# A two-block transformer on one core: the matmuls' moving operands as contiguous chunks, read and written every fourth 16-byte line in four rounds, with new gaps ahead of the two weight tiles

## The reference

```python
z = h @ w_in[l]                              # 2048 -> 10248 columns
merged = gc * (conv_y @ w_conv_out[l]) + ga * (attn @ w_attn_out[l])
x = x + merged @ w_mix_out[l]
u = jnp.square(jax.nn.relu(rmsnorm(x, g_mlp[l]) @ w_ff1[l]))   # 8192 wide
x = rmsnorm(x + u @ w_ff2[l], g_final)
...
proj = h @ w_in_2[l]                         # second block, 5648 columns
x = x + gate_m * (concat(attn, ssm) @ w_out_2[l])
x = x + gate_f * conv_ffn(h, w_up_2[l], conv_ffn_w_2[l], conv_ffn_b_2[l], w_down_2[l])
out = rms_norm(x, final_norm_g_2)
```

## Time and profile before

| | |
|---|---|
| median of 3 runs | 2444.2 us (2444.05 to 2444.67) |
| the profiled execution, its span | 2444.7 us |
| TensorE matmul (PE) busy | 2423.8 us, 99%, 14373 matmuls |
| TensorE weight load (PEld) busy | 2149.2 us, 88% |
| VectorE (DVE) busy | 1969.0 us, 81% |
| ScalarE (ACT) busy | 1261.4 us, 52% |
| GpSimd (POOL) busy | 89.1 us, 4% |
| DMA | 566.81 MB, mean 232 GB/s |

### The profile page before, as it was taken

The page is one execution under the profiler, slowest core; times in us unless marked ns, Lnnn a source line. Parts: engine busy times, 40 slices in busy tenths (PEclk is TensorE's granted clock), DMA queues, the critical chain, the costliest instruction groups (busy, mean ns, idle before and its releaser), DMA issues.

```text
span 2444.7 us, 47745 instructions
## 1 busy us (share of the span) xinstructions
PE 2423.8 (99%) x14373; PEld 2149.2 (88%) x14373; DVE 1969.0 (81%) x3114; ACT 1261.4 (52%) x2038; POOL 89.1 (4%) x109
## 2 busy tenths in 40 slices
PE   8999999999999999999999999999999999999998
PEld 7888888888888888888888988889888888888887
DVE  7778876689987887887898877776887887887886
ACT  6444445565554454554555555565545445445455
POOL 0000001000000000000000105300000000000000
PEclk9999999999999999999999999999999999999999
DMA  7786885657888888888888555555566656656555
GB/s 275 274 282 211 279 284 192 200 190 268 285 292 293 287 291 292 286 293 291 289 288 281 175 177 194 188 171 190 167 187 200 202 180 198 198 178 212 192 176 169
DMA packets 162812, 566.81 MB, mean 232 GB/s; under 512 B 18883, under 2 KB 19452, under 8 KB 162748
## 3 DMA queue, kind: packets, MB, share of 16 engines
q1 hardware_dynamic: 132572, 458.71, 56.4%
q10 hardware_dynamic: 27792, 101.20, 12.5%
q0 software_dynamic: 2384, 6.09, 1.0%
HBM read 563.51 MB, written 2.42 MB: 231 GB/s over the span
## 4 chain that ended last, share of the span: by engine, by line
PE 77%; DVE 4%; issue 2%; ACT 1%; DVEq 0%; DMA 0%; ACTq 0%; SPq 0%
PE bank L334 77%; DVE w_lo L1345 1%; DVE scratch L1994 0%; DVE scratch L1992 0%; DVE scratch L1351 0%; DVE scratch L1997 0%; ACT w_hi L823 0%; DMA w_raw<-in_w_in 0%; DVE Z L1705 0%; DVE H L1714 0%; DVE scratch L2020 0%; ACT U L1297 0%; DVE scratch L2014 0%; DVE scratch L1378 0%; PE bank L678 0%
## 5 line engine op out<-in xcount | busy, mean ns | idle before, releaser
L1345 DVE TENSOR_TENSOR w_lo<-w_raw,w_hi 128x1024 fp32r<-128x1024 f32 (+2 forms) x898 | 1048.0, 1176 | 117.1 <-ACT w_hi L823 107.5
L334 PE MATMUL bank<-H,w_hi 128*128 128x512 f32 (+1 forms) x4480 | 1100.0, 386 | 9.3 <-ACT w_hi L275 8.1
L334 PEld LDWEIGHTS bank<-H,w_hi 128*128 128x128 f32 x4480 | 799.3, 188 | 136.7 <-issue 11.2
L823 ACT ACTIVATE w_hi<-w_raw 128x1024 fp32r<-128x1024 f32 (+2 forms) x898 | 876.4, 1012 | 24.1 <-PE bank L334 8.4
L334 PEld LDWEIGHTS bank<-H,w_lo 128*128 128x128 f32 x4416 | 591.5, 188 | 40.5
L334 PE MATMUL bank<-H,w_lo 128*128 128x256 f32 x4416 | 602.9, 277 | 0.0
L334 PE MATMUL bank<-U,w_hi 128*128 128x512 f32 (+1 forms) x2011 | 501.7, 384 | 0.5 <-DVE U L2022 0.3
L853 ACT ACTIVATE scratch<-bank 128x256 f32<-128x256 f32 x355 | 135.1, 381 | 669.3 <-PE bank L334 668.7
L334 PEld LDWEIGHTS bank<-U,w_hi 128*128 128x128 f32 x2011 | 351.1, 188 | 50.0 <-DVE U L2022 0.6
L334 PEld LDWEIGHTS bank<-U,w_lo 128*128 128x128 f32 x1984 | 275.3, 188 | 23.7
L334 PE MATMUL bank<-U,w_lo 128*128 128x256 f32 x1984 | 282.1, 277 | 0.0
(11 more groups left out here) (246 smaller groups left out, 1113.2 us busy)
## 6 DMA issues: line engine op xcount, KB each, us to landing
w_raw<-in_w_ff SPq DMA_DIRECT2D x256, 512.0 KB, 5.0
ada_w<-in_w_ada ACTq DMA_DIRECT2D x192, 512.0 KB, 4.7
w_raw<-in_w_up SPq DMA_DIRECT2D x176, 512.0 KB, 4.5
w_raw<-in_w_z SPq DMA_DIRECT2D x96, 512.0 KB, 4.8
w_raw<-in_w_in SPq DMA_DIRECT2D x88, 512.0 KB, 4.4
w_raw<-in_w_gate SPq DMA_DIRECT2D x64, 512.0 KB, 4.6
w_raw<-in_w_down SPq DMA_DIRECT2D x64, 384.0 KB, 3.2
w_raw<-in_w_down SPq DMA_DIRECT2D x64, 320.0 KB, 3.4
```

Of the source, the lines that this page charges most:

```text
L334: return nc.tensor.matmul(out, lhsT, rhs, start=start, stop=stop, skip_group_check=True)
L823: A(w_hi[:, slot, 0:cols], w_raw[:, slot, 0:cols], ACT.Copy).then_inc(sem("w_high"), 1)
L1345: TT(w_lo[:, slot, 0:cols], w_raw[:, slot, 0:cols], w_hi[:, slot, 0:cols].bitcast(F32), ALU.subtract)\
```

## The change

H, U and B become plain contiguous areas of 16 chunks of 128 lines. All matmuls of `mm_lines` now walk through a chunk in four rounds: first lines 0, 4, 8 and so on, then 1, 5, 9 and so on, then from 2 and from 3; the output is walked in the same way (four numbers, skip twelve, four rounds), so that each result lands where it did. A matmul of 512 columns has rounds of 32 lines, one of 256 columns rounds of 16. Number, shape, order and semaphores of all instructions stay. H, U, B and G, Z are placed with a gap of 1024 numbers between H and U (the chains of before reached beyond the area there), and the small tiles R and ss move into that gap. Unused tiles of 11 and 6 lines stand ahead of `w_hi` and `w_lo`; a tile starts at a multiple of two lines, so the first becomes a gap of 12 lines.

```diff
-STEP = 3
 LINES = 2 * T // LINE
-CHAIN_N = NC * 2 * T + (STEP - 1) * 2 * T
+AREA_N = NC * 2 * T
+GAP = 1024
+HIGH_SPACE, LOW_SPACE = 11, 6
...
-            area = nc.alloc_sbuf_tensor_at(name, [P, CHAIN_N], F32R, offset=base + at)
-            return bass.AP(area[:, :].tensor, LINE, [[CHAIN_N, P], [2 * T, NC], [STEP * LINE, LINES], [1, LINE]])
+            area = nc.alloc_sbuf_tensor_at(name, [P, AREA_N], F32R, offset=base + 4 * at)
+            return area[:, :].rearrange("p (k l e) -> p k l e", k=NC, e=LINE)
...
-        U = chunks_by_line("U", NC * 2 * T * 4)
-        B = chunks_by_line("B", 2 * NC * 2 * T * 4)
+        U = chunks_by_line("U", AREA_N + GAP)
+        B = chunks_by_line("B", 2 * AREA_N + GAP)
...
         w_raw = sb("w_raw", [P, 4, PIECE])
+        sb("space_hi", [P, HIGH_SPACE * LINE])
         w_hi = sb("w_hi", [P, 4, PIECE], F32R)
+        sb("space_lo", [P, LOW_SPACE * LINE])
         w_lo = sb("w_lo", [P, 4, PIECE], F32R)
...
-        R = sb("R", [P, T])
-        ss = sb("ss", [P, T])
+        R = nc.alloc_sbuf_tensor_at("R", [P, T], F32, offset=base + 4 * AREA_N)
+        ss = nc.alloc_sbuf_tensor_at("ss", [P, T], F32, offset=base + 4 * (AREA_N + T))
...
+        def in_turn_of_lines(ap):
+
+            return ap.rearrange("p (i a) e -> p a i e", a=4)
...
             def mm_lines(out, lhsT, rhs, start, stop):
-                return mm(lines(out), lhsT, rhs, start, stop)
+
+                return mm(in_turn_of_lines(lines(out)), lhsT, in_turn_of_lines(rhs), start, stop)
```

More of the change, by code:

```diff
@@ L107, in build @@
         base = (nc.sbuf_base + 31) // 32 * 32
-        ctx.enter_context(nc.sbuf_tensor("arena", [P, 3 * NC * 2 * T + 1024 + (Z_BLOCKS - 32) * T], F32))
+        ctx.enter_context(nc.sbuf_tensor("arena", [P, 3 * AREA_N + GAP + (Z_BLOCKS - 32) * T], F32))
         def sb(name, shape, dt=F32):
@@ L121, in chunks_by_line @@
         def chunks_by_line(name, at):
-            area = nc.alloc_sbuf_tensor_at(name, [P, CHAIN_N], F32R, offset=base + at)
-            return bass.AP(area[:, :].tensor, LINE, [[CHAIN_N, P], [2 * T, NC], [STEP * LINE, LINES], [1, LINE]])
+            area = nc.alloc_sbuf_tensor_at(name, [P, AREA_N], F32R, offset=base + 4 * at)
+            return area[:, :].rearrange("p (k l e) -> p k l e", k=NC, e=LINE)
         H = chunks_by_line("H", 0)
-        U = chunks_by_line("U", NC * 2 * T * 4)
-        B = chunks_by_line("B", 2 * NC * 2 * T * 4)
-        G = nc.alloc_sbuf_tensor_at("G", [P, NC, 2, T], F32, offset=base + NC * 2 * T * 4 + 4096)
-        Z = nc.alloc_sbuf_tensor_at("Z", [P, Z_BLOCKS, T], F32, offset=base + 2 * NC * 2 * T * 4 + 4096)
+        U = chunks_by_line("U", AREA_N + GAP)
+        B = chunks_by_line("B", 2 * AREA_N + GAP)
+        G = nc.alloc_sbuf_tensor_at("G", [P, NC, 2, T], F32, offset=base + 4 * (AREA_N + GAP))
+        Z = nc.alloc_sbuf_tensor_at("Z", [P, Z_BLOCKS, T], F32, offset=base + 4 * (2 * AREA_N + GAP))
         X = sb("X", [P, NC, T])
```

## The result

The changed kernel takes 2483.82 us (2483.56 to 2485.14, median of 4), the kernel before 2444.43 us beside it. The ratio is 1.0162, with a 95% interval of 1.0147 to 1.0176. The forecast was 2405 us; the range, 2350 to 2535, holds the result, the sign is wrong. The profiled execution has a span of 2482.1 us. In all runs of these kernels a span is 1.7 to 1.9 us shorter than its time (here 2483.96 and 2482.1), so the profiled execution of the kernel before, with a span of 2444.7, took some 2446.5 us (an estimate), 2 us above its median; the spans of the two traces therefore differ by 2 us less than the times.

A forecast was written before the change was run, and what follows sets the result against it. TensorE's matmul pace was taken as the bound, 2345 us of 2444.7. Half of the stream's 79 us loss was taken as removed, 2444.2 - 39 = 2405 us, other parts at no cost; range 2350 to 2535.

The forecast's parts named there:

- the sign: Whole kernel: forecast faster, 2444.2 - 39 = 2405 us; chances faster 0.58, same 0.10, slower 0.32.
- distances at no price: Operand against weight tiles: distances change, no row says which is good; the 39 us forecast gain gives them no term.
- half of the stream's loss: All large matmuls: the new line order removes half of the 79 us lost along the stream, 39 us.
- `narrow` row: Matmuls with only four lines of weights, 0.227 us each: taken to show weight-load collision is not most of the loss.
- the 11.5 ns: Each 512-column matmul: 0.2248 us against 0.2133 at 2.4 GHz, a loss put down to the full pace of asking for lines.
- Reading four apart collides more: Rival, matmul reads: lines four apart meet each other and the weight load; 2450 to 2529 us, middle 2490; chance 0.24.
- `keep_warm` as the price of straight reading: Matmuls reading contiguous lines: if four apart were as bad, 0.233 us per 512 columns, 85 us together, 2529 us.
- Parts at no cost: Outside matmul pace: no instruction, wait, DMA or queue position added or moved; ScalarE and VectorE writes become contiguous; nothing.
- The pace is the same: Matmul pace in three stages: the same under different DMA, VectorE and ScalarE loads, so not set by their memory work.
- VectorE as cover: Tightest stretch: VectorE, idle 0.23 to 0.24 us a unit, can follow to about 5.2 us, covering the forecast.
- Writing in pieces: Rival, matmul result writes: 16-byte pieces cost 5% of the stream, 117 us, giving 2561 us; chance 0.08.

The follow-up runs named there:

- 11 and 11: Changed kernel with high and low weight tiles both 11 lines (modulo 16) behind the operand, as in the kernel before: 2438.14 us, ratio 0.9971.
- 8 and 14: The changed kernel itself, high weight tile 8 and low tile 14 lines (modulo 16) behind the operand, against the kernel before: 2483.82 us, ratio 1.0162.
- the streams: No block computed, TensorE runs bare matmuls over distances; halves of eight wide and eight narrow took 2687 to 2780 ns in rounds, mean 2747 in old order.
- 12 and 12: Changed kernel without the two gap tiles, both weight tiles 12 lines (modulo 16) behind the operand: 2449.70 us, ratio 1.0020.
- 12 and 11: Changed kernel with the high weight tile 12 and the low tile 11 lines behind the operand: 2423.11 us, ratio 0.9912.
- 7 and 7: Changed kernel with both weight tiles 7 lines (modulo 16) behind the operand in place of 8 and 14: 2447.63 us, ratio 1.0011.

## Why the prediction was wrong

**The part that failed: distances at no price.** The prediction said that no row told which distance was good, and then took its sum, its share of one half of the stream's loss and its forecast from the order alone. The distances were the larger term: with the new order, the step from 11 and 11 to 8 and 14 goes from 2438.1 to 2483.8 us, a loss of 46; the order, with one line of place, gains 7. In the old order the same step is 2745 - 2707 = 38 ns a half in the streams, some 33 us for 870 halves.

**Why it was waved off.** The `narrow` row, 0.227 us with loads of 16 columns, was read as "the collision with the weight load is not most of the loss". In size that is right for the old order: 10.7 ns stay with a load of 16 columns, and at distance 11 the full load adds only 0.5. But the kernel before stood at the best distance of the streams. A row from the best point shows nothing of what leaving it costs. The row was evidence on the present loss, not on the change's.

**The gain.** "Half of the stream's loss" gave 39 us, a share that no row backed. What the rounds give at the old distances is at most some 8 us, and at the best pair found 21, so this term was mis-sized as well. Of the 11.5 ns that the prediction saw in a wide matmul, 10.7 stay with short loads in the old order, and the rounds take little of that on average (223.0 against 223.9 ns with short loads). At single settings they do take it: 216.7 ns is the lowest, at distance 7 with loads of 64 columns.

**The rival that came close.** "Reading four apart collides more" was priced at 2490, middle, and 2484 came. The number is luck: its price was that of contiguous reading. It did name the changed distance to the weight tiles as a reason for it, and that is what came. That four apart is the worse order is not so: over all pairs the mean half is 2725 against 2747 ns, and one line of distance, from 12 and 12 to 12 and 11, is worth 27 us (2449.7 and 2423.1). That a short weight load takes the effect of the distance away, as a collision would have it, is shown for the old order alone.

**Terms that held.** `keep_warm` as the price of straight reading: 0.233 us assumed, 233.3 ns measured in the changed layout; 4.1 ns assumed for the narrow ones, 117.3 - 114.3 = 3.0 measured; so 2529 us forecast, 2519 measured. Some of that is luck, since straight reading takes 226.7 to 234.1 ns, by distance. Parts at no cost: counts and waits stayed, ScalarE's busy time grew by 3 us. The pace is the same with 287 and with 175 GB/s beside it. VectorE as cover: in the kernel of 2423 us TensorE's waits are still the 8.1 us and small ones.

**The rules cited.** Writing in pieces costs nothing: straight reading takes 233.3 ns with either output. So of the Trainium skill, Advanced Engine Details and Errata, Memory Cachelines, the clause on pairs of elements fits the streams, and the clause that any non-contiguous pattern slows matmuls doesn't hold for pieces of 16 bytes. The other, of the Trainium skill, SBUF — State Buffer, Who interferes with whom, that the moving operand and the weight load have independent read ports, by which their distance would count for nothing, doesn't fit: with the load cut from 128 to 16 columns the wide stream at distance 12 goes from 230.0 to 224.0 ns.

**What stays open.** That the distances made the loss is shown; the mechanism behind them is not, least of all in rounds, where short loads leave the spread as it is. Open too: what has a period of 16 lines, why the place counts beside the distance, what the order alone is worth in a whole kernel, and why the gaps in rounds wander from matmul to matmul while those of the kernel before are all alike. Only orders and pairs named here were tried; 2423 us is the best found, not a floor.

## What to carry to other kernels

When matmuls with a weight load each run back to back and nothing waits, the start addresses of weights and operands are a setting like any other: sweep them by 16-byte lines over 16 lines, in one kernel of bare streams that have the real mix of shapes and the operands at the real place, since the sum over streams of one shape was 16 to 35 us off here. After any edit to the layout, work out the distances as allocated, not as asked for: a gap of 11 lines that became 12 was the whole loss. A kernel that has been moved about for long may sit at the best of its settings, and a row taken there says nothing of what the neighbours cost.

## What was not expected of the hardware

- The distance between operand and weights acts modulo 16 lines of 16 bytes, on matmuls of float32r at the full granted clock, by up to 10 ns of 220 in four rounds. At half the clock, the 256-column matmuls of before took 0.214 us, against 0.213 for 256 columns at 1.2 GHz.
- The pace of a matmul depends on its neighbours: at distances 7 and 7 the streams of one kind took 220.1 and 113.3 ns, the same matmuls eight by eight in the kernel 225.7 and 114.0.
- Moving operand and weights together by one line changes single paces by up to 6.6 ns in the old order and 9.2 in rounds, and moving them by five lines does the same as by one, within 0.2 ns (in rounds from distance 3 on).
- Reading lines five apart takes 266.7 ns for 512 columns at every distance, three apart 224.5 to 230.4.
